# One block of a two-part transformer on one core: a recurrent mixer's decay levels one projected tile later, its tail inside the attention

## The reference, cut to what matters

```python
h = h + 0.5 * rmsnorm_2(swiglu(rmsnorm_2(h, norm_g[0]), ffn1_gu, ffn1_down), norm_g[1])
z = rmsnorm_2(h, norm_g[2]) @ w_in
hq, hf, hi, hg, aq, ak, av, su, sv = jnp.split(z, idx, axis=-1)
o_a = hgrn2(hq, hf, hi, lb)
o_a = rmsnorm_2(o_a, hg_norm_g) * jax.nn.sigmoid(hg...)
o_b = swa_sink_attention(aq, ak, av, sinks, pos)
o_c = spatial_gating(su, sv, sg_ln_g, sg_w, sg_b)
mixed = jnp.concatenate([o_a, o_b, o_c], axis=-1) @ w_out
h = h + rmsnorm_2(mixed, norm_g[3])
```

## Time and profile before

| what | value |
|---|---|
| median of three executions | 2761.98 us (2761.33 to 2762.87) |
| the profiled execution's own time | 2762.42 us |
| its span | 2760.6 us |
| TensorE busy, mean granted clock | 95%, 0.979 |
| VectorE, ScalarE, GpSimd busy | 40%, 36%, 47% |
| DMA engines, mean | 85 GB/s |
| mixer stage of layer 0, lead tiles' end to the attention's first rotation | about 1047 to 1165 us |
| attention of layer 0 | 1165 to 1219 us |

### The profile page before, as it was taken

One profiled execution on the slowest core, in us unless ns is written; L12 is line 12 of the kernel. 1 busy time (PEld: TensorE's weight loads), 2 busy tenths in 40 slices (PEclk: granted clock), 3 DMA queues, 4 the chain that ended last, 5 costly groups with the idle time before them and its releaser, 6 DMA issues. The chain is left out here.

```text
span 2760.6 us, 33708 instructions
## 1 busy us (share of the span) xinstructions
PE 2621.1 (95%) x12468; PEld 2107.1 (76%) x12468; DVE 1108.4 (40%) x1679; ACT 1001.7 (36%) x1484; POOL 1287.4 (47%) x1664
## 2 busy tenths in 40 slices
PE   6999999899999999989999999999999989999997
PEld 3788767677888877767888877888877757888885
DVE  5588654544222027545222036322017554322015
ACT  5223323334332233454233235332234454333234
POOL 1333456455555544345545445555544335545543
PEclk8999999999999999999999999999999999999999
DMA  6222111032333322102332322323322202332322
GB/s 264 69 62 83 57 41 32 23 111 88 99 95 101 94 84 75 62 25 83 100 99 92 99 92 77 107 92 100 99 92 69 68 16 84 100 99 92 99 92 77
DMA packets 63335, 234.05 MB, mean 85 GB/s; under 512 B 7264, under 2 KB 7520, under 8 KB 62688
## 3 DMA queue, kind: packets, MB, share of 16 engines
q1 hardware_dynamic: 61056, 222.33, 25.3%
q10 hardware_dynamic: 2144, 9.80, 0.9%
HBM read 230.00 MB, written 2.10 MB: 84 GB/s over the span
## 5 line engine op out<-in xcount | busy, mean ns | idle before, releaser
L423 POOL TENSOR_TENSOR wlo<-raw,whi 128x256 fp32r<-128x256 f32 x1584 | 1174.7, 774 | 1305.8 <-ACT whi L524 1305.8
L1814 PE MATMUL banks<-xhi,whi 128*128 128x512 f32 x1984 | 777.7, 392 | 0.0
L1815 PE MATMUL banks<-xhi,wlo 128*128 128x512 f32 x1984 | 772.8, 389 | 0.0
L1824 PE MATMUL banks<-xlo,whi 128*128 128x512 f32 x2016 | 760.9, 393 | 9.5 <-DVE xlo L1106 9.4
L524 ACT ACTIVATE whi<-raw 128x1024 fp32r<-128x1024 f32 x396 | 415.4, 1054 | 359.8 <-PE banks L1824 359.1
L1824 PEld LDWEIGHTS banks<-xlo,whi 128*128 128x128 f32 x2016 | 378.1, 189 | 97.8 <-DVE xlo L1106 17.1
L1814 PEld LDWEIGHTS banks<-xhi,whi 128*128 128x128 f32 x1984 | 372.9, 188 | 82.0 <-issue 2.8
L1815 PEld LDWEIGHTS banks<-xhi,wlo 128*128 128x128 f32 x1984 | 372.8, 188 | 78.2 <-issue 1.5
L1815 PE MATMUL banks<-act_hi,wlo 128*128 128x512 f32 x704 | 273.9, 389 | 0.0
L1814 PE MATMUL banks<-act_hi,whi 128*128 128x512 f32 x704 | 273.9, 389 | 0.0
L1824 PE MATMUL banks<-act_lo,whi 128*128 128x512 f32 x704 | 273.9, 389 | 0.0
(11 more groups left out here) (400 smaller groups left out, 3110.5 us busy)
## 6 DMA issues: line engine op xcount, KB each, us to landing
raw<-in_stream SPq DMA_DIRECT2D x396, 512.0 KB, 3.5
ada_raw<-in_stream SPq DMA_DIRECT2D x24, 512.0 KB, 7.2
h<-in_x ACTq DMA_DIRECT2D x2, 2048.0 KB, 12.3
out<-h SPq DMA_DIRECT2D x4, 512.0 KB, 2.6
ctx_raw<-in_ctx ACTq DMA_DIRECT2D x1, 1024.0 KB, 19.6
dft_t<-in_dft_t ACTq DMA_DIRECT2D x1, 1024.0 KB, 4.8
ple_raw<-in_ple ACTq DMA_DIRECT2D x2, 512.0 KB, 3.5
mixpar<-in_mixpar ACTq DMA_DIRECT2D x2, 384.0 KB, 4.2
```

The source lines that it names most:

```text
L423: piece = pool.tensor_tensor(wlo[:, i, s], raw[:, i, s], whi[:, i, s].bitcast(F32), ALU.subtract)
L1814: pe.matmul(acc[acc_of[t]][:], whi[:, u % SLOTS, i], x_h, start=(k == 0), stop=False, skip_group_check=split)
L1815: pe.matmul(acc[acc_of[t]][:], wlo[:, u % SLOTS, i], x_h, start=False, stop=False, skip_group_check=split)
L1824: mm = pe.matmul(acc[acc_of[t]][:], whi[:, u % SLOTS, i], x_l, start=False, stop=(k == k_tiles - 1), skip_group_check=leading and m < leads)
```

## The change

All of it is in the mixer stage, in both layers.

- TensorE: `hgrn_step` does nothing after tile 6; scores n come after tile 6 + n, and every later step of the mixer one tile later too, so the sums of squares come after tile 17, directly ahead of the attention.
- VectorE: `hgrn_level(n)` begins with the merge of level n - 1 and forms the decays after it. Tile 6 is taken after level 1, and from there tile 6 + n after level n. `gating_center` moves into level 7. `hgrn_out` moves from before tile 17 into the attention, after the probabilities of block 0.
- ScalarE: from level 2 on the decays come behind the wait for tile 4 + n; the gelu comes ahead of level 7; the sigmoid follows the gelu, which leaves one table load less per layer; `hgrn_high` moves into the attention, after the copy of block 1.
- The inverse roots get a place of their own, `hg_inverse`, over `k_tok`, since the attention's first scores lie over `k_dec`.

```diff
+        hg_inverse = at("hg_inverse", MX + 28 * KB, [2, SEQ])
...
             def hgrn_norm(layer):
-                inverse_root(*(((layer, "hg", g), 64, bank[4 + g], k_dec[:, g]) for g in range(2)))
-                act.activation(z[:, 6:8], z[:, 6:8], ACT.Sigmoid).then_inc(*done("hg_act", ("hg_out_gate", layer)))
-                log_and_exp()
+                inverse_root(*(((layer, "hg", g), 64, bank[4 + g], hg_inverse[:, g]) for g in range(2)))
...
                     if 1 <= i <= 16:
                         turned(i - 1)
+                    if i == 2:
+                        hgrn_high(layer)
...
                 act.activation(z[:, 8:12], z[:, 8:12], ACT.Gelu_apprx_tanh).then_inc(*done("sg_act", ("gelu", layer)))
+                act.activation(z[:, 6:8], z[:, 6:8], ACT.Sigmoid).then_inc(*done("hg_act", ("hg_out_gate", layer)))
                 log_and_exp()
...
                         hgrn_logs(layer)
-                        for n in range(1, len(LEVELS) + 1):
+                        hgrn_decays(layer, 1)
+                        projected(5)
+                        for n in range(2, len(LEVELS)):
+                            projected(4 + n)
                             hgrn_decays(layer, n)
-                            projected(4 + n)
-                        hgrn_chunk_decays(layer)
+                        projected(11)
                         gating_gelu(layer)
+                        hgrn_decays(layer, len(LEVELS))
                         projected(12)
                         gating_squares(layer)
                         projected(13)
-                        hgrn_tokens(layer)
+                        hgrn_chunk_decays(layer)
                         inverse_root(((layer, "ln"), 2 * P, acc[3][:], tmp[2][:]))
                         projected(14)
+                        hgrn_tokens(layer)
                         projected(15)
-                        hgrn_out(layer)
                         gating_tokens(layer)
                         projected(16)
+                        hgrn_out(layer)
+                        projected(17)
                         hgrn_norm(layer)
-                        projected(17)
                         gating_high(layer)
-                        hgrn_high(layer)
                         attention(layer)
...
                 b = LEVELS[n - 1]
-                if n == 1:
-                    v.wait_ge(*after("hg_step", ("hg_cleared", layer)))
+                hgrn_masked(layer, n - 1)
+                if n == len(LEVELS):
+                    gating_center(layer)
                 v.wait_ge(*after("hg_exp", (layer, n)))
-                v.wait_ge(*after("hg_scores", (layer, n - 1)))
...
-                hgrn_masked(layer, n - 1)
...
+                    if i == 1:
+                        hgrn_out(layer)
...
                         for n in range(1, len(LEVELS) + 1):
                             hgrn_level(layer, n)
-                            projected(5 + n)
+                            if n == 1:
+                                projected(6)
+                            projected(6 + n)
                         hgrn_chunk(layer)
-                        gating_center(layer)
-                        projected(13)
+                        projected(14)
                         gating_scale(layer)
-                        projected(14)
+                        projected(15)
                         hgrn_states(layer)
-                        projected(15)
                         projected(16)
                         gating_out(layer)
-                        hgrn_out(layer)
                         projected(17)
                         attention(layer)
...
-                levels = len(LEVELS) + 1
-                if 5 <= m < 5 + levels:
-                    hgrn_scores(layer, m - 5)
+                levels = len(LEVELS) + 2
+                if m == 5 or 6 < m < 5 + levels:
+                    hgrn_scores(layer, 0 if m == 5 else m - 6)
```

More of the change, by code:

```diff
@@ L1222, in hgrn_out @@
                     v.wait_ge(*after("hg_act", ("hg_o_copied", (layer, g))))
-                    v.tensor_tensor(hg_o[:, g], hg_o[:, g], k_dec[:, g], ALU.mult)\
+                    v.tensor_tensor(hg_o[:, g], hg_o[:, g], hg_inverse[:, g], ALU.mult)\
                         .then_inc(*done("hg_step", ("hg_normed", (layer, g))))
```

## The result

The changed kernel takes **2767.26 us** (median of 17 runs, 2766.35 to 2768.52); the kernel before, on the same chips, takes 2761.98 us (17 runs, 2760.11 to 2764.35). The ratio is 1.0019, with a 95% interval of 1.0013 to 1.0026. That is 5.3 us more, inside the 0.2% that I called no change, right at its slower edge. The forecast was 2766.5 us, its range 2760.5 to 2771.5.

What follows compares the result with a forecast made beforehand. TensorE, busy 95% of the span, was taken as the bound. Per layer -0.3 - 0.5 + 0.15 + 2.9 = +2.25 us, for two layers +4.5 us, gave 2766.5 us on the median; range 2760.5 to 2771.5.

Steps and rivals of the forecast that it cites:

- The stall in front of tile 7: Mixer level 1: TensorE's wait passes from the merge to GpSimd's weights; tile 7 starts at 1070.0, gain 0.3 us per layer.
- rival D: Mixer level 1: a port lock runs GpSimd and VectorE in series, tile 7 at 1071.0, total 2768.5 us; chance 0.08.
- 0.6 us lost per us of overlap: Mixer level 1: rate at which VectorE's operations slow GpSimd's weight pieces; 2.6 us of overlap costs 1.6 us.
- The gelu's 0.5 us: Mixer gating: the gelu comes a level earlier, so TensorE's wait at the gating's sum goes, 0.5 us per layer.
- The roots' wait: Attention start: the third rotation waits for the inverse roots to read its bank, 0.0 to 0.2 us, taken as 0.15.
- `hgrn_out` in the attention: Attention: 2.9 us of VectorE ahead of block 1's reciprocal delay TensorE's turn of block 1 by all 2.9 us.
- `hgrn_high` at zero: Attention: two ScalarE copies ahead of block 3's exponentials cost nothing, upper bound 1.1 us.
- Rival B: Attention: the delay is absorbed, only -0.65 us per layer is left, total 2760.7 us; chance 0.10.
- no slack stands behind block 1 up to block 4: Attention: TensorE is busy without a gap up to block 4, so nothing takes back the 2.9 us delay.
- The clock: Attention, turns of blocks 1 to 5: when the clock comes back decides 1.4 us either way, zero as the middle.
- rival C: Attention, turns of blocks 1 to 5: added idle time holds the clock down longer, 1.4 us per layer, 2769.3 us; chance 0.20.
- Rival A: Mixer: tile 7's weights are there, so it starts at 1064.8; -5.15 us per layer, 2751.7 us in all; chance 0.07.

Runs made afterwards that it cites:

- e2: Changed kernel with `hgrn_out` in halves in VectorE's attention blocks 5 and 7, `hgrn_high` and the low parts behind: 2764.01 us, ratio 1.0007.
- e6: Changed kernel with `hgrn_high` moved from ScalarE's third attention block to its eighth, the low parts behind it: 2769.73 us, ratio 1.0025.
- e10: Changed kernel with `hgrn_out` in halves in attention blocks 3 and 4, `hgrn_high` in ScalarE's blocks 4 and 6, low parts in 5 to 8: 2762.90 us.
- e5: Kernel before with the attention's part of the change alone (`hg_inverse`, `hgrn_out` behind block 0's probabilities, `hgrn_high` in ScalarE's third block): 2768.73 us, ratio 1.0024.
- e1: Changed kernel with ScalarE's cast of tile 7's weights ahead of level 1's decays: 2755.01 us, ratio 0.9973.
- e9: Changed kernel with the weights' cast ahead of level 1's decays and VectorE's copy of tile 5 ahead of the cumulation: 2752.76 us, ratio 0.9965.
- e3: Changed kernel with the early weights' cast, and `hgrn_out` in halves in attention blocks 5 and 7 with its high and low parts behind: 2753.21 us.
- e8: Changed kernel with early weights' cast, tile 5's copy ahead of the cumulation, and `hgrn_out` in halves in attention blocks 3 and 4, high/low parts later: 2749.26 us.
- e4: Kernel before with the weights' cast ahead of level 1's decays, as a control: 2765.53 us, ratio 1.0012.
- e7: Changed kernel with level 1's decays ahead of the merge of level 0 on VectorE, as in the kernel before: 2767.18 us, ratio 1.0017.

## Why the prediction was right, and where it was not

The total was 0.8 us off, and that close it came by luck: terms made up for each other, and one of them lies outside the change. The places and the releasers were right. Against the sum, per layer:

**The stall in front of tile 7: right in place and cause, close in size by luck.** I had its start at 1070.0, or 12.96 us after scores 0. It came 12.37 us after them in layer 0 and 13.47 in layer 1, 12.92 in the mean. But layer 0 is the exception: in e2, e6 and e10, whose code here is the same, tile 7 starts 13.45 to 13.53 us after scores 0 in all six layers, halfway to rival D (13.96 us). So 0.6 us lost per us of overlap was too little. GpSimd's four pieces, 2.79 us undisturbed, lost 2.0 us in seven of the eight layers, and 0.9 in one, where I took 1.6. VectorE's two decays beside them took 1.25 + 1.21 us in layer 0 and 0.68 + 1.22 in layer 1, where 0.69 is usual: the loss is shared between the two engines, and the same code shares it out either way. That is why D's sum did not come: only GpSimd's share was on TensorE's path. The lock of D agrees in kind.

**The gelu's 0.5 us: right.** No wait stands at the gating's sum. These two terms together were -0.8; the mixer stage gave -1.49 and -0.60, -1.0 in the mean. (From level 2 on 2.06 + 2.6 + 1.3 is 5.96 us and not the 6.3 that I wrote; nothing waited there, so nothing hung on it.)

**The roots' wait: right in place, too small.** The row shows 0.19 us where I took 0.15. But the third rotation begins 2.07 us after the first (1164.57 - 1162.50), where four of ten matmuls in 4.45 us take 1.8, and e10, which has this part and not the early tail, has the turn of block 1 at 17.2 against 16.8. It costs about 0.4 us, more than the idle time that the row names.

**`hgrn_out` in the attention: right.** Forecast 2.9 us in full; e5 alone shows 3.0, and 0.4 + 3.0 is what the turn of block 1 is late. I had `hgrn_high` at zero, and e6 bears it out to within 0.2 us. Rival B, the delay absorbed, is out: the turn came 3.5 us later and nothing gave it back. But the sentence that no slack stands behind block 1 up to block 4 was wrong: it looked at TensorE's gaps, and the slack is VectorE's, 2.1 us ahead of block 4's maximum. It takes back no delay of TensorE; it is where the same work costs little, as e10 showed.

**The clock: mis-sized.** I took zero as the middle of 1.4 us either way and looked only between the turns of blocks 1 and 5. That stretch was 11.8 us in both layers, against 13.0 and 11.6 before, so rival C as I had put it did not happen: its mark was above 13. (In layer 1 the clock was back 27 us after the first rotation and not 23, as C would have it, but the stretch grew by no more than 0.3 us for it.) The cost came later. From the turn of block 5 to the output projection it was 25.9 us in both layers against 24.2 and 25.3, with the clock down again around 1206 in layer 0 and as far behind the rotations in layer 1. Other layers bear out that this is the clock (table in the last section): 24.2 us is what the stretch takes without such a fall, 25.3 with one at its end and 25.9 with one in its middle. Over the whole attention behind the turn of block 1 that is +0.55 and +0.92 us, 0.7 in the mean. So the step "zero as the middle" failed, in its size and in its place.

**The sum.** Forecast +2.25 per layer; measured -1.05 + 4.2 = +3.15, the 0.9 more being 0.3 of roots, 0.1 of `hgrn_out`, 0.7 of clock, less 0.2 in the mixer. Two layers make +6.3 us. The total came out near +4.5 only because scores 0 began 1.1 us earlier in the profiled execution, and the medians differ by the same 5.3 us as the two profiled executions. That is luck. Over the kernels here it began anywhere from 1055.5 to 1059.4 us, with the same code ahead of it; why was not tried.

**Rival A** was rightly kept out of the range: the weights were not there. It gave 2751.7 us for the case that they are. With the weights there, e1 took 2755.01; e9, which also frees the bank in time, took 2752.76.

## What to carry to other kernels

When work is moved up to hide a wait, list everything that it needs, its weights and its buffers too, and when each is ready: a wait that goes from one releaser to another is no gain, and one line that frees the second may be worth more than the whole move (here 12 us, and none without the move). When work is moved into a pipelined stage, find the block in which the engine waits in the trace; 3 us of VectorE cost 3 us ahead of block 1, next to nothing in blocks 3 and 4, and 1.3 us in blocks 5 and 7. And when a sum of small terms comes out right, check the terms by distances between marks inside the stage, not by the total.

## What the runs showed of the hardware

The clock of TensorE falls again inside the attention, and where it does moves with edits that leave those blocks alone. In the changed kernel it is at the lower of its two levels, 1.2 GHz, from about 1206.3 to 1209.7 us:

```profile
1204.00:1206.00 2.00, 1.67 (x14) 1.07 (x13) 1.19 (x6) 1.47 (x7) 0.92 (x1) 1.00 0.00 0
1206.00:1208.00 2.00, 1.83 (x12) 1.37 (x12) 0.69 (x5) 0.91 (x5) 1.16 (x2) 0.58 0.00 0
1208.00:1210.00 2.00, 2.00 (x12) 1.15 (x9) 0.00 (x0) 0.63 (x5) 0.00 (x0) 0.57 0.00 0
```

In the two us before it fell TensorE was busy 1.67 of 2.00 us, with waits of 0.43 and 0.50 us for GpSimd ahead of two turns. No wait of the 17 us that it had been at 2.4 GHz, since 1189.2, was longer than 0.51 us, in either layer. Windows of one us over the attention of all twelve kernels, 24 stages, show the first low stretch end 23 to 30 us after the first rotation (27 in both layers of the changed kernel, 26 and 23 before), and then 19 further falls of 3 to 7 us, in 17 stages: two in layer 0 of e3 and in layer 1 of e8, none in seven stages, among them both of e2 and layer 0 of the kernel before. The other layer of the kernel before has one, near its end. They come about 17 us after the clock had come back (nine), or about 27 (eight), or 7 (two). What a fall costs is read from one stretch of the stage, the turn of block 5 to the output projection, in the kernels whose work in it is that of the kernel before and of the changed one:

| further fall of the clock | turn of block 5 to output projection, us |
|---|---|
| none | 24.16 (before layer 0, e4 layer 1, e5 layer 0), 24.34 (e9 layer 0) |
| one at the end, 50 to 55 us after the first rotation | 25.3 to 25.4 (before layer 1, e1 both, e7 layer 1) |
| one in the middle, at 40 to 44 us | 25.9 (changed both, e4 layer 0, e5 layer 1, e7 layer 0, e9 layer 1) |

A fall in the middle, low for 3.4 us, costs 1.6 to 1.8 us, one at the end about 1.1 us inside the stage. The one of 6.8 us in layer 0 of e6 goes with 27.8 us, where e6's other layer, without one, has 24.6. The Trainium skill ("TensorE: Matmul & The Clock Gate", "Part 1: The HAM clock gate") says that activity over a free-running window decides; that the same instructions meet a fall in one layer and none in the other fits a rule of that kind. Which difference brings a fall was not tried and stays open. It fits what is missing in e3 and e8, where the same stretch takes 28.0 us in layer 0 of e3 (two falls) against 25.4 in e2 (none), and 26.9 in layer 1 of e8 against 25.6 in its layer 0. It sets how far a forecast of this stage can be trusted, by some 2 us per layer.

GpSimd's pieces and VectorE's operations with two inputs in SBUF hold each other up: GpSimd's pieces went from 0.73 to 1.17, 1.26 and 1.71 us, VectorE's from 0.69 to 1.21 or 1.25, eight scans from 2.63 to 4.55. Which of them pays can vary from layer to layer in one execution, as in the changed kernel, though seven of eight layers with this code paid alike.
